# A hybrid encoder step on one core: scatters, score loads, the lag of the dense sums, and the second attention are changed

## The reference, cut to what matters

```python
proj = x @ w_in                                   # q, k, v, latents, gates
...
s = s * ((MLA_NOPE_DIM + MLA_ROPE_DIM) ** -0.5)   # second attention (MLA)
mask = (k_pos // CHUNK)[None, :] <= (q_pos // CHUNK)[:, None]
p = jax.nn.softmax(jnp.where(mask, s, NEG_INF), axis=-1)
return jnp.einsum('bhqk,bkhd->bqhd', p.astype(v.dtype), v)
...
merged = sigmoid(g_a) * (o_a @ w_oa) + sigmoid(g_b) * (o_b @ w_ob)
h = layer_norm(ALPHA * x + merged @ w_out, ln1_g, ln1_b)
y = layer_norm(ALPHA * h + peer(h), ln2_g, ln2_b)
```

## Time and profile before

| | us |
|---|---|
| median of three runs | 3550.9 (3545.1 to 3551.59) |
| profiled execution, its own time | 3558.26 |
| its span | 3556.5 |
| PE busy | 3036.3 (85%) |
| DVE busy | 2536.0 (71%) |
| POOL busy | 1558.1 (44%) |
| ACT busy | 1210.2 (34%) |
| group 0, six blocks | 0 to 437.2 |
| group 1, six blocks | 437.2 to 1172.8 |
| group 2, six blocks | 1172.8 to 2041.3 |
| dense | 2041.3 to 3556.5 |

### The profile page before, as it was taken

One profiled execution on the slowest core, in us unless ns is written; L12 is line 12 of the kernel. 1 busy time (PEld: TensorE's weight loads), 2 busy tenths in 40 slices (PEclk: granted clock), 3 DMA queues, 4 the chain that ended last, 5 costly groups with the idle time before them and its releaser, 6 DMA issues. The chain is left out here.

```text
span 3556.5 us, 36144 instructions
## 1 busy us (share of the span) xinstructions
PE 3036.3 (85%) x10170; PEld 1717.7 (48%) x10170; DVE 2536.0 (71%) x5041; ACT 1210.2 (34%) x3181; POOL 1558.1 (44%) x1184
## 2 busy tenths in 40 slices
PE   8979989676889895775887898999989999989988
PEld 5755745344545453433654554444444444444443
DVE  0122069887786877877867678888888888788886
ACT  0241234665533435754552322222222222222221
POOL 0000025667662288888777533333333333333330
PEclk9989999785789997997688999999999999999999
DMA  4675589666799997576678999999999999999995
GB/s 144 217 254 177 190 311 394 207 181 202 222 321 359 338 341 218 145 202 181 183 248 301 406 404 399 399 405 396 404 378 412 400 407 398 397 393 407 400 408 204
DMA packets 375912, 1098.51 MB, mean 309 GB/s; under 512 B 91712, under 2 KB 210208, under 8 KB 289568
## 3 DMA queue, kind: packets, MB, share of 16 engines
q0 software_dynamic: 165072, 751.05, 56.6%
q1 hardware_dynamic: 176800, 303.85, 24.4%
q10 hardware_dynamic: 33840, 41.30, 3.3%
HBM read 1031.97 MB, written 63.02 MB: 308 GB/s over the span
## 5 line engine op out<-in xcount | busy, mean ns | idle before, releaser
L428 POOL DMA_INDIRECT expert_rows<-in_experts,picked_index x640 | 770.9, 1204 | 1271.1 <-DVE ff_sum L583 1157.1
L571 DVE SCALAR_TENSOR_TENSOR expert_rows<-expert_rows,h_tile 128x1024 f32<-128x1024 f32 x672 | 820.1, 1220 | 256.8 <-DMA expert_rows<-in_experts,picked_index 212.4
L583 DVE SCALAR_TENSOR_TENSOR ff_sum<-expert_rows,coefficients,ff_sum 128x1024 f32<-128x1024 f32 x672 | 860.8, 1281 | 92.2 <-ACT coefficients L534 75.9
L1786 PE MATMUL dense_act_ps<-dense_hT,key_columns 128*128 128x384 f32 x2048 | 724.7, 510 | 139.5 <-DMA key_columns<-in_key_columns 128.5
L451 POOL DMA_INDIRECT gates_by_expert<-dense_gate,gate_address x384 | 680.3, 1772 | 154.7 <-issue 129.2
L1775 PE MATMUL dense_out_ps<-dense_value_rows,dense_weights 128*128 128x512 f32 x1536 | 678.9, 592 | 0.5 <-DVE dense_weights L1854 0.5
L1786 PEld LDWEIGHTS dense_act_ps<-dense_hT,key_columns 128*128 128x128 f32 x2048 | 399.4, 198 | 482.8 <-DMA key_columns<-in_key_columns 196.2
L833 PE MATMUL proj_ps<-xT,w_in_block 128*128 128x384 f32 (+1 forms) x1392 | 424.1, 468 | 40.7 <-PEq L1595 16.5
L1775 PEld LDWEIGHTS dense_out_ps<-dense_value_rows,dense_weights 128*128 128x128 f32 x1536 | 291.8, 190 | 342.6 <-issue 309.7
L833 PEld LDWEIGHTS proj_ps<-xT,w_in_block 128*128 128x128 f32 x1392 | 268.3, 193 | 195.7 <-issue 37.9
L528 ACT ACTIVATE activated<-dots 128x1 f32<-128x1 f32 (+1 forms) x631 | 124.8, 198 | 638.5 <-DVE expert_rows L571 601.5
(11 more groups left out here) (186 smaller groups left out, 3144.8 us busy)
## 6 DMA issues: line engine op xcount, KB each, us to landing
key_columns<-in_key_columns SPq DMA_DIRECT2D x128, 512.0 KB, 11.6
dense_value_rows<-in_experts SPq DMA_DIRECT2D x128, 512.0 KB
gates_by_expert<-zeros POOLq DMA_DIRECT2D x12, 2048.0 KB, 21.9
wq_half<-in_peer_wq SPq DMA_DIRECT2D x48, 512.0 KB
dense_gates<-gates_by_expert SPq DMA_DIRECT2D x128, 192.0 KB
w_in_block<-in_w_in ACTq DMA_DIRECT2D x18, 1024.0 KB
w_in_block<-in_w_in SPq DMA_DIRECT2D x18, 1024.0 KB
w_out<-in_w_out SPq DMA_DIRECT2D x24, 512.0 KB, 7.5
```

What stands on the lines that cost most here:

```text
L428: pool.indirect_dma_start(to, None, self.a["experts"], bass.IndirectOffsetOnAxis(ap=index[:, k:k + 1], axis=0)).then_inc(self.got[p % self ...
L571: dve.scalar_tensor_tensor(place, place, 1.0, self.h[n % 2][:], ALU.mult, ALU.mult, accum_out=self.dots[:, s % TOPK:s % TOPK + 1]).then_in ...
L583: dve.scalar_tensor_tensor(total, self.ring[:, p % self.RING, D:2 * D], self.coef[:, y % TOPK:y % TOPK + 1], total, ALU.mult, ALU.add).the ...
L1786: mm = nc.tensor.matmul(up[it % 2][:, 0:W], keys[it % KB][:, k, :], hTd[:, k, :], start=(k == 0), stop=(k == KC - 1))
```

## The change

1. The numbers of scatters in SHARES change, and the dealing: an event's credit goes by VectorE's work in it (a row counts four, a stage of ranking one), and no more than one is kept. By the events, the scatters of project, stick, mla_project, mla, merge and scores go from 15, 38, 16, 34, 25, 0 to 11, 38, 16, 34, 24, 5 in group 1, and from 55, 73, 26, 54, 32, 16 to 30, 64, 22, 60, 24, 36 in group 2; 20 come in dense, where none were, the last at event 33 of 726.
2. ScalarE issues the loads of scores: the first two of a group at the start of project or dense (`first_loads`), the others as soon as head r-2 has its indices (`act_index`).
3. In dense LAG is 14: the sums and the loads of gates and values come six turns later, and there are 19 buffers of weights instead of 13.
4. `mla_attend`: three buffers of scores, two heads ahead; the scale with a minus sign goes into the gain of the query latents (`mla_project`), so one minimum takes the place of maximum and negation; transposes in parts of at most four through a buffer of one bank; products with v for two heads together, v as the stationary operand, so that the output comes out transposed and one copy of ScalarE brings it to obT. The division by the sums moves to `merge_norm`: the inverse sums are transposed, spread by eight matmuls that pick a head's row, and multiplied onto obT ahead of the first matmuls that read it.

```diff
-        ((2, "project"), 40, 1, 9, 44), ((2, "stick"), 26, 2, 6, 72), ((2, "mla_project"), 7, 1, 2, 26), ((2, "mla"), 25, 2, 5, 70),
-        ((2, "merge"), 20, 1, 2, 48), ((2, "scores"), 29, 1, 0, 40),
...
+        ((2, "project"), 40, 1, 9, 44), ((2, "stick"), 26, 2, 6, 64), ((2, "mla_project"), 7, 1, 2, 22), ((2, "mla"), 25, 2, 5, 60),
+        ((2, "merge"), 20, 1, 2, 24), ((2, "scores"), 29, 1, 0, 36),
+        ((3, "dense"), 1000, 1, 24, 60),
...
-        self.scores_at, self.h_at, self.scatter_at = {}, {}, {}
+        self.scores_at, self.scores_after, self.h_at, self.scatter_at = {}, {}, {}, {}
         for r, (t, h) in enumerate(self.routes):
-            k = max(k_of["route", r - 1, 0] if r >= 2 else 0, opened[home[t]])
-            assert k <= k_of["route", r, 0], (r, t, h)
+            if r >= 2 and k_of["route", r - 2, self.INDEX_AFTER] >= opened[home[t]]:
+                self.scores_after[r - 2] = r
+                continue
+            k = opened[home[t]]
+            assert points[k][1] == 0 and points[k][0][1] in ("project", "dense") and k <= k_of["route", r, 0], (r, t, h)
             self.scores_at.setdefault(key(k), []).append(r)
...
-        share = {block: gates / min(len(self.beside[block]), 90) for block, _, _, _, gates in self.SHARES}
+        work = lambda e: 4.0 * e[2] if e[0] == "rows" else 1.0
+        share = {block: gates / min(sum(work(e) for e in self.beside[block]), 280.0) for block, _, _, _, gates in self.SHARES}
         for k, (block, i, e) in enumerate(points):
-            credit += share[block]
+            credit += share[block] * work(e)
             while waiting and credit >= 1:
                 credit -= 1
                 self.scatter_at.setdefault(key(k), []).append(waiting.pop(0))
-            credit = min(credit, 4.0)
+            credit = min(credit, 1.0)
...
+    def first_loads(self, act):
+        for r in self.scores_at.get((self.block, 0), []):
+            self.load_scores(act, r)
+
...
-            pool.wait_ge(self.fine, self.count[r - 2, 1])
+            act.wait_ge(self.fine, self.count[r - 2, 1])
...
-        pool.dma_start(self.sc[r % 2][:].rearrange("p c n -> p (c n)"), self.a["peer_scores"][t * HEADS + h]).then_inc(self.sc_in[r % 2], 16)
+        act.dma_start(self.sc[r % 2][:].rearrange("p c n -> p (c n)"), self.a["peer_scores"][t * HEADS + h]).then_inc(self.sc_in[r % 2], 16)
...
+        if r in self.scores_after:
+            self.load_scores(act, self.scores_after[r])
...
+            nc.vector.tensor_scalar(gain[:, 0:QC], gain[:, 0:QC], -MLA_SCALE, None, ALU.mult).then_inc(gain_scaled, 1)
+            dve.wait_ge(gain_scaled, 1)
...
-        sp = [s.enter_context(nc.psum_tensor(f"score_ps{i0 + i}", [P, 1024], F32)) for i in range(2)]
-        tp = s.enter_context(nc.psum_tensor(f"probsT_ps{g.n}", [P, 1024], F32))
-        op = s.enter_context(nc.psum_tensor(f"mla_out_ps{g.n}", [P, 512], F32))
+        sp = [s.enter_context(nc.psum_tensor(f"score_ps{3 * g.n + i}", [P, 1024], F32)) for i in range(3)]
+        tp, op = banks(nc, s, f"mla_ps_turned{g.n}_", 2)
+        parts = lambda i: [keys_of(i)[2][c:c + 4] for c in range(0, len(keys_of(i)[2]), 4)]
+        copies_before = [sum(len(parts(i)) for i, _ in items[:n]) for n in range(N + 1)]
...
+            scores(0)
+            scores(1)
+            for n in range(N + 1):
+                if n + 2 < N:
+                    scores(n + 2)
+                if n < N:
                     i, h = items[n]
...
+                    for y, part in enumerate(parts(i)):
+                        if n or y:
+                            pe.wait_ge(t_copied, copies_before[n] + y)
+                        for x, (off, rows, vt) in enumerate(part):
+                            mm = nc.tensor.transpose(tp[0:rows, P * x:P * x + r], p[n % 2][0:r, off:off + rows], m["ident"][0:r, 0:r])
+                        mm.then_inc(t_done, 1)
+                k = n - 1
+                if k >= 0 and k % 2:
+                    i, h = items[k]
+                    r, tiles = rows_of(i), keys_of(i)[2]
+                    pe.wait_ge(t_copied, copies_before[k + 1])
...
                     for x, (off, rows, vt) in enumerate(tiles):
-                        mm = nc.tensor.matmul(op[0:r, HD * h:HD * (h + 1)], pT[n % 2][0:rows, P * x:P * x + r],
-                                              f["mv"][0:rows, vt, HD * h:HD * (h + 1)], start=(x == 0), stop=(x == len(tiles) - 1),
-                                              skip_group_check=True)
+                        for par in range(2):
+                            first = HD * (h - 1 + par)
+                            mm = nc.tensor.matmul(op[half[par], P * (h // 2):P * (h // 2) + r], f["mv"][0:rows, vt, first:first + HD],
+                                                  pT[(k - 1 + par) % 3][0:rows, P * x:P * x + r], start=(x == 0), stop=(x == len(tiles) - 1),
+                                                  skip_group_check=True)
                     mm.then_inc(av_done, 1)
-                n = t - 3
-                if 0 <= n < N and items[n][1] == HEADS - 1:
...
-                    nc.scalar.activation(p[t % 2][0:r, 0:nk], sp[t % 2][0:r, 0:nk], ACT.Exp, bias=nm[0:r, t:t + 1],
-                                         scale=MLA_SCALE, accum_out=rs[0:r, t:t + 1]).then_inc(p_done, 1)
+                    nc.scalar.activation(p[t % 2][0:r, 0:nk], sp[t % 3][0:r, 0:nk], ACT.Exp, bias=nm[0:r, t:t + 1],
+                                         scale=-1.0, accum_out=rs[0:r, t:t + 1]).then_inc(p_done, 1)
...
+                    if n >= 3:
+                        act.wait_ge(av_done, (n - 3) // 2 + 1)
+                    for y, part in enumerate(parts(i)):
+                        act.wait_ge(t_done, copies_before[n] + y + 1)
+                        if i < TILES:
+                            nc.scalar.copy(pT[n % 3][:, 512 * y:512 * y + P * len(part)], tp[:, 0:P * len(part)]).then_inc(t_copied, 1)
...
+                n = t - 2
+                if n >= 0 and items[n][1] == HEADS - 1:
+                    i = items[n][0]
+                    r = rows_of(i)
+                    act.wait_ge(av_done, (n + 1) // 2)
+                    nc.scalar.copy(f["obT"][:, :, g.at[i]:g.at[i] + r], op[:].rearrange("p (x q) -> p x q", x=4)[:, :, 0:r]).then_inc(o_copied, 1)
+                bg.act(min(1.0, t / N))
...
-                    nc.vector.reduce_max(mx[0:r, t:t + 1], sp[t % 2][0:r, 0:nk], AX).then_inc(max_done, 1)
-                    dve.wait_ge(max_done, t + 1)
-                    nc.vector.tensor_scalar(nm[0:r, t:t + 1], mx[0:r, t:t + 1], -MLA_SCALE, None, ALU.mult).then_inc(nm_done, 1)
+                    nc.vector.tensor_reduce(nm[0:r, t:t + 1], sp[t % 3][0:r, 0:nk], AX, ALU.min).then_inc(nm_done, 1)
...
-                    nc.vector.tensor_tensor(on[turn(i) % 2][0:r, :].rearrange("p (h d) -> p h d", h=HEADS),
-                                            op[0:r, :].rearrange("p (h d) -> p h d", h=HEADS),
-                                            ri[0:r, at].unsqueeze(2).broadcast_to([r, HEADS, HD]), ALU.mult).then_inc(on_done, 1)
...
+            for n, t in enumerate(g.tiles):
+                r = rows_of(t)
+                mm = nc.tensor.transpose(ps[4][0:HEADS, g.at[t]:g.at[t] + r], ri[0:r, HEADS * n:HEADS * (n + 1)], m["ident"][0:r, 0:r])
+            mm.then_inc(ri_turned, 1)
...
                 for i, o in enumerate((f["oaT"], f["obT"])):
+                    if j == 0 and i == 1:
+                        pe.wait_ge(ri_copied, 1)
+                        for q in range(4):
+                            for par in range(2):
+                                pick = m["ident"][0:HEADS, 2 * q + par:2 * q + par + 1].broadcast_to([HEADS, HD])
+                                mm = nc.tensor.matmul(ps[q][HD * par:HD * par + HD, 0:W], pick, riT[0:HEADS, :], start=True, stop=True, skip_group_check=True)
+                            mm.then_inc(spread, 1)
+                        pe.wait_ge(scaled, 4)
...
+            act.wait_ge(ri_turned, 1)
+            nc.scalar.copy(riT[0:HEADS, :], ps[4][0:HEADS, 0:W]).then_inc(ri_copied, 1)
...
+            for q in range(4):
+                dve.wait_ge(spread, q + 1)
+                nc.vector.tensor_tensor(f["obT"][:, q, :], f["obT"][:, q, :], ps[q][:, 0:W], ALU.mult).then_inc(scaled, 1)
...
-        LAG, AHEAD = 8, 2
+        LAG, AHEAD = 14, 2
         KB, VB, GB, AB = 5, 5, 4, LAG + 5
...
             wait_for_scores(act, m, len(GROUPS))
+            bg.first_loads(act)
```

130 lines of the change are left out of this document (45 added, 85 removed).

## The result

The changed kernel has a median of 3563.15 us over 20 runs (3554.26 to 3573.56) against 3557.54 for the kernel before (20 runs); the ratio is 1.0024, 95% interval 1.0014 to 1.0034 (the two medians alone give 1.0016). The forecast was 3532 and a range of 3492 to 3560, so both the sign and the range were missed, the range by 3 us. The forecast started from 3550.9, the median of three runs; over twenty the kernel before is 6.6 us slower, and the same differences from there would give 3538 and a range up to 3567. What is clearly missed is the sign. The profiled execution took 3564.5 us and spans 3562.7, 6.2 more than before. Its table of stages answers to the earlier trace rows; the columns are the same.

A forecast was written before the change was run, and what follows sets the result against it. The prediction took DMA to bound dense, the merges and scores(2), and GpSimd's queue to limit project(2) and mla(2). Block terms and +12 for dense summed to -19 from 3550.9, giving 3532 us, range 3492 to 3560.

The forecast's parts named there:

- Project(2): Group 2's project block: fewer scatters and no loads on GpSimd let late rows pass faster, -16 us [-22, -6].
- mla(1): Group 1's mla block: the second attention removes VectorE work and waits for outputs, transposes and scores, -12 us [-15, 0].
- mla(2): Group 2's mla block: GpSimd sets the end and has 162 us of work against 174.0, -11 us [-14, 0].
- Stick(2): Group 2's stick block: 26 us leave GpSimd's queue but VectorE waits for ScalarE, -3 us [-10, 0].
- mla_project(2): Group 2's mla_project block: GpSimd begins late without a backlog, so the change costs, +4 us [-8, +8].
- Merge(2): Group 2's merge block: fewer scatters give -6, normalising costs about 3, together -3 us [-9, +3].
- Scores(2): Group 2's scores block: GpSimd becomes the last engine and leaves a tail of scatters, +9 us [0, +15].
- (a) The start: Dense's start: the first gates and keys behind them wait for the last scatter, +21 us [+8, +52].
- (b) The end: Dense's end: the longer lag leaves no first matmuls and the same ten tiles of sums, -9 us [-18, +5].
- Rival 1: Dense's start: last scatter lands beyond 100 us, costing +52 instead of +21; kernel 3563 us, chance 0.13.
- Rival 2: Mla blocks: one transpose bank and TensorE's low clock leave a third of the attention's gain; kernel 3550 us, chance 0.13.
- Rivals 3 and 4: Rival 3: dense start cheap, dense -7, 3502 us, chance 0.20; rival 4: GpSimd stays last, project(2) -6, 3550, chance 0.07.

The follow-up runs named there:

- the lag alone: The kernel before with only the sums in dense 14 tiles behind instead of 8: ratio 1.0048 to the kernel before, dense 1533.5 us.
- the attention alone: The kernel before with only the second attention and the normalising in merge of the changed kernel: 3549.96 us, ratio 0.9973 to the kernel before.

## Why the prediction was wrong

**Right.** Project(2): -19.7 for -16, and by the mechanism named. TensorE ends 7.75 us before the block instead of 22.95, 23 late rows (46 records) pass in 105 us with the DMA engines at 1.07, against 22 in 122.3 us. Part of the size is luck: by the trace 48 scatters became 29 in this block, 19 fewer where the sum took 25, and the ten loads, priced at 12 us of GpSimd, show no gain in the run that moves them:

```profile
1350.41 3.79 PE L939 MATMUL log_weight_ps<-sb_qT,sb_kT 64*128 64x128 f32 x32 [7.75 <-PEq L697]
```

```profile
1240.00:1345.00 105.00, 28.12 (x46) 0.98 1.07 401
```

mla(1): -11.0 for -12. The waits of the earlier trace rows for outputs and for their transposes, 10.3 us, are gone from VectorE's table, and its busy time fell by 8.6 us, for some 6. The third wait, for scores, is still there (5.2 us for 4.1), in spite of the third buffer; the table has this one line from 835 us to the block's end:

```profile
DVE score_ps L1380 <- PE score_ps L1299: 5.2, 3, 2.3
```

mla(2): -7.2 for -11, and GpSimd's queue fills it to the microsecond (139.42 busy and 27.4 of gaps make 166.8). Stick(2), +0.3 for -3, belongs to ScalarE, for which VectorE waits 18.2 us (18.1 before). The products by pairs take 94 ns of busy time each at a clock of 0.74, for 164 at 0.73, and the sum got nothing from it, as mla(2) did not wait for TensorE:

```profile
1593.70:1760.50 166.80, 31.71 (x336) 27.86 (x336) 0.74 0.63 179
```

This agrees with the exchange that the Trainium skill describes ("TensorEngine Tiling (Array Packing)", Performance Considerations); what a change of mode costs, no run here measures.

**Wrong in size, with little effect.** mla_project(2): -10.9 for +4. GpSimd did begin late, but only 19 instructions lie in the block, five of them fetches; the rest of the 22 scatters slid into mla(2), whose -7 contains them. Merge(2): -14.9 for -3; VectorE's waits for rows there are gone. Scores(2): +18.4 for +9; VectorE waits 31.3 us for rows there, 8.8 before. Scores(1): -6.5 for +1, where runs with the same code differ by 4. Group 0: +1.4 for -3, its merge 5.7 us longer. Together the blocks ahead gave 48 us, not 31.

**Wrong: dense, +54 for +12.** This is the term that failed, in both of its parts, and with it the sign.
- *(a) The start*, +21 in the sum, is 28 (against the run with the same lag and none dealt to dense) to 36 (against the lag alone). The mechanism was right, and SyncE's queue, turn 10, the 11 tiles and the standing TensorE came as described. I had priced it as DMA time lost between 60 and 80 us after the start. But GpSimd brought four scatters along and came to dense's own 14.5 us late, the last one went out at 86 us, not 68, the rate sank before that (290 GB/s), and above all I left out what comes after the pause: TensorE has to catch up, for 40 us at 263 GB/s, and ScalarE, VectorE and the rows behind it wait meanwhile.
- *(b) The end*, -9 in the sum, became a loss: the lag cost dense 13 to 18 us, 12 of them at the end. (The figures given for the -9, 3 x 5.16 less one tile of keys, 1.3 us at 400 GB/s, make -14.) I counted the tiles of sums left at the last row as "the same ten". There were 12 and a wait, since TensorE's turns were then tied to VectorE's rows. I had treated first matmuls and sums as work that could be exchanged; the first matmuls were what TensorE did while VectorE was late.

The other 13 us of dense came in the runs with ScalarE's loads, priced at nothing, and with the dealing, which had no term there. Whether they cost that, and how, stays open.

Rival 1 named 3563, and the measured time is 3563.15. That is chance in good part: it put dense at +43 and the blocks at -31, and both were exceeded, and it stood for +12 from 3550.9, where the change is +6 to +9 from 3557.54. What it said of leftovers from scores(2) came true. Its condition, a last scatter that lands beyond 100 us, was not met: SyncE went on at 91 us, and that was enough. Rival 2 is excluded by the attention alone (mla(1) 109.2). Its mechanism was there: TensorE's waits for ScalarE's copies grew from 26.8 to 49.1 us in mla(2) and from 21.9 to 32.1 in mla(1); but GpSimd's queue sets the length of mla(2), and mla(1) lost its 11 us all the same. Of its clock: TensorE's granted clock in mla(1) went up from 0.60 to 0.69 while its busy time went down from 95 to 76 us, so less work did not leave it slower here. As I had read the Trainium skill's page "TensorE: Matmul & The Clock Gate" (Part 1), that activity releases the throttle, it should have gone down or stayed; the trace decides. Rivals 3 and 4 fell: the start was not cheap, though project(2) came near what rival 3 had for it, and GpSimd let go of project(2).
